# Computing the gMLP v projection tile by tile inside the norm loop, in an eight-core decoder layer

## What is computed

```python
h = rmsnorm(x, g_mix)
proj = h @ w_in                       # 1024 -> 3584
a = proj[..., :512]                   # pooling branch
z = gelu(proj[..., 512:1536])         # u: 512..1023, v: 1024..1535
u, v = z[..., :512], rmsnorm(z[..., 512:], g_v)
s = tril(w_s) @ v (per chunk of 128 tokens and group) + b_s
merged = gate_a * (pool(a) @ w_pool_out) + gate_b * ((u * s) @ w_gmlp_out)
x = x + merged @ w_out
x = x + (silu(h2 @ w_gate) * (h2 @ w_up)) @ w_down    # h2 = rmsnorm(x, g_ffn)
y = rmsnorm(x, g_final)
```

## Time and profile before

| | |
|---|---|
| median of 3 runs | 941.32 us (940.83 to 941.81) |
| the profiled execution | 941.41 us |
| its span on the slowest core (core 5) | 939.9 us |
| spans of the 8 cores | 933.0 to 939.9 us |
| PE busy | 858.1 us, 91% of the span |
| DVE, ACT, POOL busy | 360.4, 239.0, 151.4 us |

### The profile page before, as it was taken

How to read it: one execution, slowest core, us unless ns; L and a number is a source line. 1 busy time by engine, 2 the same in 40 slices (tenths; PEclk the granted TensorE clock), 3 DMA queues, 4 the chain that set the end, 5 groups by cost and what they waited for, 6 DMA issues and landing times.

```text
span 939.9 us, 13183 instructions; the slowest of 8 cores (933.0 to 939.9 us)
## 1 busy us (share of the span) xinstructions
PE 858.1 (91%) x4648; PEld 403.2 (43%) x4648; DVE 360.4 (38%) x594; ACT 239.0 (25%) x440; POOL 151.4 (16%) x174
## 2 busy tenths in 40 slices
PE   0589999998999999999972799999989999999996
PEld 0344444444444444444422344444444444444442
DVE  1584234447212112153456562343462212223446
ACT  2336222216221111100035272222072111110003
POOL 4202011015101100000034020110240110100004
PEclk9999999999999999999995899999989999999998
DMA  8992336676475573465489025366764646535404
GB/s 223 168 136 23 47 35 77 79 97 74 50 85 66 70 89 45 70 90 64 71 210 241 1 26 66 51 85 89 91 81 54 85 56 85 79 51 84 79 1 180
DMA packets 101795, 78.84 MB, mean 84 GB/s; under 512 B 5276, under 2 KB 96788, under 8 KB 101715
## 3 DMA queue, kind: packets, MB, share of 16 engines
q0 software_dynamic: 93936, 57.97, 48.2%
q1 hardware_dynamic: 6958, 19.31, 6.5%
q10 hardware_dynamic: 837, 0.72, 0.3%
HBM read 127.41 MB, written 9.01 MB: 145 GB/s over the span
## 4 chain that ended last, share of the span: by engine, by line
PE 83%; DMA 6%; DVE 4%; POOL 3%; issue 2%; ACT 1%; DVEq 0%; POOLq 0%; ACTq 0%; SPq 0%
PE ps L338 79%; DMA ring<-w_in 4%; POOL rs L356 2%; DMA yp<-ybuf 2%; PE ps L603 1%; PE ps L387 1%; PE ps L600 1%; DVE hb L375 1%; DVE shr L470 1%; DVE shr L474 1%; DVE shr L478 1%; DVE ovl L487 0%; ACT junk L347 0%; DVE ms L352 0%; ACT hT L395 0%
## 5 line engine op out<-in xcount | busy, mean ns | idle before, releaser
L338 PE MATMUL ps<-hT,ring 128*128 128x512 bf16 (+1 forms) x2720 | 503.7, 341 | 3.1 <-DMA ring<-w_in 3.1
L338 PEld LDWEIGHTS ps<-hT,ring 128*128 128x128 bf16 x2720 | 229.1, 98 | 263.4 <-issue 15.5
L338 PE MATMUL ps<-ring,ovl 128*128 128x512 bf16 (+1 forms) x1020 | 223.6, 379 | 0.0
L721 DVE TENSOR_TENSOR ovl<-ftmp,ps 128x512 bf16<-128x512 f32 (+1 forms) x110 | 62.4, 583 | 257.2 <-PE ps L338 250.9
L338 PEld LDWEIGHTS ps<-ring,ovl 128*128 128x128 bf16 (+1 forms) x1020 | 97.7, 97 | 120.7 <-issue 5.6
L714 ACT ACTIVATE ftmp<-ps 128x512 f32<-128x512 f32 (+1 forms) x110 | 56.6, 514 | 249.5 <-PE ps L338 249.5
L347 ACT ACTIVATE junk<-xbuf 128x1024 bf16<-128x1024 f32 (+1 forms) x51 | 53.7, 1054 | 203.5 <-DVE xbuf L741 139.3
L741 DVE TENSOR_TENSOR xbuf<-xbuf,ps 128x512 f32<-128x512 f32 (+1 forms) x102 | 70.0, 686 | 81.2 <-PE ps L338 81.2
L356 POOL TENSOR_TENSOR rs<-ms,mhalf 128x1 f32<-128x1 f32 (+1 forms) x68 | 64.5, 951 | 142.9 <-DVE ms L352 142.8
L387 PE MATMUL ps<-ident_b,hb 128*128 128x128 bf16 (+1 forms) x272 | 27.4, 262 | 60.9 <-DVE ms L352 43.4
L338 PE MATMUL ps<-ovl,ring 128*128 128x512 bf16 (+1 forms) x320 | 63.2, 337 | 0.0
(11 more groups left out here) (71 smaller groups left out, 375.6 us busy)
## 6 DMA issues: line engine op xcount, KB each, us to landing
ring<-w_gate POOLq DMA_DIRECT2D x22, 512.0 KB, 8.7
ring<-w_up POOLq DMA_DIRECT2D x22, 512.0 KB, 10.7
xbuf<-xp SPq DMA_DIRECT2D x16, 512.0 KB, 10.5
ring<-w_in POOLq DMA_DIRECT2D x16, 512.0 KB, 9.4
ring<-w_down POOLq DMA_DIRECT2D x8, 1024.0 KB, 9.6
yp<-ybuf SPq DMA_DIRECT2D x16, 512.0 KB, 5.6
ring<-w_in POOLq DMA_DIRECT2D x6, 1024.0 KB, 24.1
ring<-w_out POOLq DMA_DIRECT2D x4, 1024.0 KB, 13.1
```

What stands on the lines that cost most here:

```text
L338: ins = e.matmul(out=out, lhsT=lhs_fn(i), rhs=rhs_fn(i), start=(i == 0), stop=(i == n - 1))
L721: P.op('dve', lambda e, bU=bU, fi=fi, f=f, c0=c0, W=W: e.tensor_tensor(out=actT[:, f, c0:c0 + W], in0=ftmp[:, fi, :W], in1=PS[bU][:, :W], ...
```

## The change

It does four things.

- `blocks`: in each half the v block (`cb` = 2) is first, then a (0), then u (1). Before it was a, v, u.
- The v stage is gone as a stage. Its work is added to the norm pipeline as three more steps with lags 4, 5 and 6: `c1` (projection, gelu, square), `c2` (L352, L356), `c3` (product into `vtok`). The v block is released after the last tile, and `ws_prep` follows.
- `pipeline` goes through the steps of a round from the last to the first. This holds for all three places that use it.
- `b4_list[g]()` is called after group g of the u stage.

```diff
         for s in range(NSUP):
-            for cb in (0, 2, 1):
+            for cb in (2, 0, 1):
                 blocks.append([(0, 8, 512, win_v[:, :, cb * 512:(cb + 1) * 512])])
...
             for i in range(n + max(lags)):
-                for si, lag in enumerate(lags):
-                    t = i - lag
+                for si in reversed(range(len(lags))):
+                    t = i - lags[si]
                     if 0 <= t < n:
                         steps[t][si]()
...
-            pipeline([norm_stages(slot, R, col0, gmix_rep, 'gmix') for (slot, R, col0) in tts], [0, 1, 2, 3])
+            cj, cslot, cres_ = ring_next()
+            wvC = slot_view(cslot, 0, 8, 512)
+            steps = []
+            for (slot, R, col0) in tts:
+                ns = norm_stages(slot, R, col0, gmix_rep, 'gmix')
+                box = {}
+
+                def c1(slot=slot, R=R, col0=col0, box=box, wvC=wvC, cres_=cres_):
+                    b = bank()
+                    P.op('pe', mm_group(PS[b][:R, :],
+                                        lambda i: hT[:, i, col0:col0 + R],
+                                        lambda i: wvC[:, i, :], 8),
+                         reads=cres_ + hT_res([slot]), writes=[('ps', b)])
+                    fi = nxt('ft', 2)
+                    P.op('act', lambda e: e.activation(out=ftmp[:R, fi, :], in_=PS[b][:R, :],
+                                                       func=AF.Gelu_apprx_tanh),
+                         reads=[], writes=[('ftmp', fi), ('ps', b)])
+                    k, sq, rsf = rstd_stages(ftmp[:R, fi, :], R, 512, [('ftmp', fi)])
...
+                    sq()
+
+                def c2(box=box):
+                    box['rsf']()
+
+                def c3(slot=slot, R=R, box=box):
...
+                        P.op('dve', lambda e: e.scalar_tensor_tensor(
+                            out=vtok[:R, slot, :], in0=ftmp[:R, fi, :], scalar=rs[:R, k:k + 1], in1=gv_rep[:R, :],
+                            op0=ALU.mult, op1=ALU.mult),
+                             reads=[('ftmp', fi), ('rs', k), 'gv'], writes=[('vtok', slot)])
...
+                steps.append(ns + [c1, c2, c3])
+            pipeline(steps, [0, 1, 2, 3, 4, 5, 6])
+            ring_release(cj)
             if s == 0:
                 ws_prep()
...
-            cj, cslot, cres_ = ring_next()
-            wv = slot_view(cslot, 0, 8, 512)
-            for ti, (slot, R, col0) in enumerate(tts):
...
-                if ti % 2 == 1 and ti // 2 < 4:
-                    b4_list[ti // 2]()
-            ring_release(cj)
-
             dj, dslot, dres = ring_next()
...
                              reads=['stmp', ('ftmp', fi)], writes=[('sgT', g, c0)])
+                b4_list[g]()
             ring_release(dj)
```

More of the change, by code:

```diff
@@ L436, in build_nc @@
             t0 = s * TPS
-            pipeline([norm_stages(slot, R, col0, gmix_rep, 'gmix') for (slot, R, col0) in tts], [0, 1, 2, 3])
+            cj, cslot, cres_ = ring_next()
[15 more added lines that the diff above has]
+                    k, sq, rsf = rstd_stages(ftmp[:R, fi, :], R, 512, [('ftmp', fi)])
+                    box['fi'] = fi
+                    box['k'] = k
+                    box['rsf'] = rsf
+                    sq()
+                def c2(box=box):
+                    box['rsf']()
+                def c3(slot=slot, R=R, box=box):
+                    fi = box['fi']
+                    k = box['k']
+                    if slot < 8:
+                        P.op('dve', lambda e: e.scalar_tensor_tensor(
+                            out=vtok[:R, slot, :], in0=ftmp[:R, fi, :], scalar=rs[:R, k:k + 1], in1=gv_rep[:R, :],
+                            op0=ALU.mult, op1=ALU.mult),
+                             reads=[('ftmp', fi), ('rs', k), 'gv'], writes=[('vtok', slot)])
+                    else:
+                        P.op('dve', lambda e: e.scalar_tensor_tensor(
+                            out=vout[:R, :], in0=ftmp[:R, fi, :], scalar=rs[:R, k:k + 1], in1=gv_rep[:R, :],
+                            op0=ALU.mult, op1=ALU.mult),
+                             reads=[('ftmp', fi), ('rs', k), 'gv'], writes=['vout'])
+                        P.op('dve', lambda e: e.tensor_copy(out=vtok[:R, slot, :], in_=vout[:R, :]),
+                             reads=['vout'], writes=[('vtok', slot)])
+                        P.dma('sp', lambda e: e.dma_start(out=nvs[:, :], in_=vout[:NSMP, :]), 'omisc',
+                              reads=['vout'])
+                steps.append(ns + [c1, c2, c3])
@@ L549, in build_nc @@
                       reads=['npsbuf'])
-            cj, cslot, cres_ = ring_next()
-            wv = slot_view(cslot, 0, 8, 512)
-            for ti, (slot, R, col0) in enumerate(tts):
-                b = bank()
-                P.op('pe', mm_group(PS[b][:R, :],
-                                    lambda i, col0=col0, R=R: hT[:, i, col0:col0 + R],
-                                    lambda i, wv=wv: wv[:, i, :], 8),
-                     reads=cres_ + hT_res([slot]), writes=[('ps', b)])
-                fi = nxt('ft', 2)
-                P.op('act', lambda e, b=b, fi=fi, R=R: e.activation(out=ftmp[:R, fi, :], in_=PS[b][:R, :],
-                                                                   func=AF.Gelu_apprx_tanh),
-                     reads=[], writes=[('ftmp', fi), ('ps', b)])
-                k = rstd_chain(ftmp[:R, fi, :], R, 512, [('ftmp', fi)])
-                if slot < 8:
-                    P.op('dve', lambda e, fi=fi, R=R, k=k, slot=slot: e.scalar_tensor_tensor(
-                        out=vtok[:R, slot, :], in0=ftmp[:R, fi, :], scalar=rs[:R, k:k + 1], in1=gv_rep[:R, :],
-                        op0=ALU.mult, op1=ALU.mult),
-                         reads=[('ftmp', fi), ('rs', k), 'gv'], writes=[('vtok', slot)])
-                else:
-                    P.op('dve', lambda e, fi=fi, R=R, k=k: e.scalar_tensor_tensor(
-                        out=vout[:R, :], in0=ftmp[:R, fi, :], scalar=rs[:R, k:k + 1], in1=gv_rep[:R, :],
-                        op0=ALU.mult, op1=ALU.mult),
-                         reads=[('ftmp', fi), ('rs', k), 'gv'], writes=['vout'])
-                    P.op('dve', lambda e, R=R, slot=slot: e.tensor_copy(out=vtok[:R, slot, :], in_=vout[:R, :]),
-                         reads=['vout'], writes=[('vtok', slot)])
-                    P.dma('sp', lambda e: e.dma_start(out=nvs[:, :], in_=vout[:NSMP, :]), 'omisc', reads=['vout'])
-                if ti % 2 == 1 and ti // 2 < 4:
-                    b4_list[ti // 2]()
-            ring_release(cj)
             dj, dslot, dres = ring_next()
```

## The result

| | before | changed |
|---|---|---|
| median | 941.56 us (10 runs) | 977.28 us (9 runs) |
| profiled execution | 941.41 us | 979.42 us |
| its span, slowest core | 939.9 us (core 5) | 977.3 us (core 1) |
| mean of the 8 spans | 936.0 us | 969.5 us |

What follows compares the result with a forecast made beforehand. It took the chain of waits as the bound, with PE waiting for every copy in the fused loop. Terms 14.9 + 3.5 (second half 4.3 less 0.8) + 2.4 + 0 = +20.8 us on 941.41 gave 962 us, range 950 to 983.

Steps and rivals of the forecast that it cites:

- the clock rival: Fused loops: PE's clock falls in the waits, +2.0 us per low tile; half the tiles low gives 979 us; chance 0.20.
- first half, to the merge: First half's fused loop, a and u stages: u stage ends at 123.9 instead of 108.94, +14.9 us, bounds 12 and 17.
- second half, to the merge: Second half's fused loop, a and u stages: u stage ends at 585.5 against 581.2, +4.3 us.
- end of the first half: First scaling there no longer stands behind an addition and starts earlier: about 0.8 us comes back.
- w_out, both halves: Reversed w_out pipelines: period 2.28 against PE's 2.34, a gain against a slower start; 0, between -2 and +2 us.
- last block, end: Last block of w_down: scaling waits for the mean just made, period 2.28 instead of 1.87 us; +2.4 us.
- The loop's step: Fused loop: PE waits for every copy; a tile takes 3.36 us with a DVE copy, 4.49 with an ACT copy.
- The hidden norm stage: First half: norm stage costs nothing before, under the weight transfer; the new loop starts at 40.4 with one tile transposed.
- The clock: Fused loops: low clock counted only at the start, 2.8 us in the first half and 2.4 in the second.
- The stall moved into the u stage: First half's u stage: PE runs out of banks waiting for DVE's pooling, 3.1 us, replacing the v stage's 3.45 us stall.
- The rival that copies are hidden: Fused loops: copies run ahead of PE, a tile costs 2.34 us, total 938.5 us; chance 0.07.

Runs made afterwards that it cites:

- e2: Kernel before, with the w_pool matmuls called after each group of the u stage instead of in the v stage: 940.54 us, ratio 1.0008.
- e5: Changed kernel, order still reversed, with projection, second and third fused steps one round later (lags 5, 6, 7): 952.98 us.
- e10: Changed kernel, order still reversed, with all copies into hT of the fused loop on DVE: 959.92 us.
- e6: Changed kernel with 4 filler matmuls of 512 columns, read by nobody, ahead of each tile's projection: 968.42 us.
- e1: Kernel before, with only the order of steps in a pipeline round reversed, at all three places: 954.6 us, ratio 1.0159.
- e3: Changed kernel with the load of gv_rep on a semaphore of its own: ratio 1.0391 to the kernel before, against 1.0385 without the edit.
- e12: Kernel before, v projection fused only in the second half, forward with c3 first, w_pool in the u stage in both halves: 934.75 us, ratio 0.9929.

## Why the prediction was right, and where it was wrong

The sign, the two main terms and their order were right, and 977.3 lies in the range of 950 to 983. But the forecast's own value, 962, was 15 us short, and the result is outside of its own bounds of 951 to 970. The range held only because it was stretched for the clock rival, which had a chance of 0.20, against the forecast's 0.71. Term by term, in the means of the table:

| term | forecast | measured | of it |
|---|---|---|---|
| first half, to the merge | +14.9 | -1.2 + 20.7 = +19.5 | clock 2.6 |
| second half, to the merge | +4.3 | +10.6 | clock 6.2 |
| end of the first half | -0.8 | -0.2 | |
| w_out, both halves | 0 | +1.0 + 1.0 | |
| last block, end | +2.4 | +1.6 | |
| sum | +20.8 | +33.5 | the slowest core +37.4 |

Of the 12.7 us between the sums 8.8 are the clock, as the filler run measures it, about 2 are w_out, and about 2 more lie in the first half, where the u stage of core 1 took 32.26 us and not the 30.5 of the sum. The 4 us by which the slowest core lost more than the mean belong to no step of the sum; 2.5 of them are its first projection, which started at 42.95 and not at 40.40. These starts scatter between cores in kernels with an unchanged front too (34.2 to 43.9 in e2).

- **The loop's step.** Right at the full clock: 3.36 and 4.49 us computed, 3.27 and 4.46 found. e5 and e10 show that what exceeds PE's own work in it is the wait for the copy.
- **The hidden norm stage.** Right. PE stood 20.5 us for the weights with one tile transposed, and in no order did the first half come below 78 us.
- **The clock.** This is the step that failed: the forecast put the low clock in the loop at nothing beyond the start, 2.8 and 2.4 us. I wrote "No row here shows a swing, so I give it 0.20". It swung: behind the first, 3 of the 8 projections of the first half's loop were wholly or partly at the low level, and 6 of 7 in the second half's; the loops' PEclk was 0.83 and 0.72. The filler run measures it at 9 us. The rival's price, half of the tiles low and 979 us, came close to the total by luck: its +17 for the clock was twice what was measured, and the total got there with other terms. Its mark (PEclk under 1 between 45 and 76 us) was the right one to look at. The Trainium skill, TensorE: Matmul & The Clock Gate, "A second HAM failure mode: psum-queue depth-cycling", describes a kernel in which PE idles briefly and often between groups of matmuls and its clock swings between the two levels. The trace agrees, with 0.72 and 0.83 where PE paused in every step and 0.98 once the pauses were filled. By that page the clock belonged into the forecast.
- **The stall moved into the u stage.** Right in size (3.1 forecast, 2.81 found), slightly wrong in place: PE stood ahead of the first `w_pool` matmul and not at a projection that had no bank. What I left out is the low clock behind it, a projection of 3.23 us; the u stage took 32.26 us, not 30.5.
- **The second half.** With the clock held up (e6) it is +4.4 where +4.3 was forecast. That is closer than its terms deserve: the measured value holds the gelu's table load of 1.28 us, which the sum did not have. The low clock adds 6.2.
- **w_out.** Forecast as 0 between -2 and +2 for both halves, found +2.0: at the bound. The period is as forecast, 2.3 us per tile on core 1; it is the slower start that was sized too small. The first tile's mean stands ahead of the second addition now and waits for ACT's square, so the second addition starts 2.50 us behind the first (238.73 to 241.23), where it started 1.72 behind it before (214.43 to 216.15):

```profile
241.12 0.15 DVE L352 TENSOR_SCALAR ms<-ss 128x1 f32<-128x1 f32 x1 [1.70 <-ACT junk L347]
```

- **The end.** +1.6 for +2.4. The period is 2.21 us, not 2.28, and the power beside an addition takes 0.55 us, as taken. The Trainium skill, GPSIMD Engine Reference, Specifications, says that POOL contends with a DVE instruction that has two inputs in SBUF. The trace agrees: 0.55 us beside an addition with one input in PSUM, 1.47 beside a scaling.
- **The rival that copies are hidden** (0.07) was refused by the order on PE, and the trace shows a wait at every projection.
- I had not asked what the reversed order costs the norm stage by itself. It is 6.6 us in the second half (e1). The sum for the fused loop did contain it, since the copy stood on the path there anyway.

What stays open: a gain of a microsecond or so from the semaphore of its own (e3) would not be seen in the scatter between cores, and whether `w_pool` in the u stage helps beside the fused second half (e12).

## What to carry to other kernels

Before work is fused into a pipeline, ask what that pipeline is hidden behind: the first norm stage was free under a weight transfer, and the same fusion that gains 4 us in the second half loses 8 to 21 in the first. In a software pipeline a lag counts only if something else stands between producer and consumer in the consumer's queue; reversed rounds take that slack away, one more round gives it back. And where PE is left with short pauses in each step, the clock belongs into the sum and not only into a rival.

## What the runs showed of the hardware

- The clock fell in a loop in which pauses of 0.94 us stood in turn with longer ones, mostly 1.7 to 3.3 us, and rose again within it: 8 matmuls of 512 columns took 1.89, 2.64, 3.00 and 3.57 us in one loop. 4 matmuls more per step, which nobody reads, made the second half's stretch 6.2 us shorter.
- A change of ACT's table cost 1.28 us (534.10 to 535.40), and in the changed kernel's second half it stood on PE's path.
- In e10, with pauses of 0.94 to 1.26 us in each step of the second half's loop, the granted clock was 1.00 on seven cores and 0.96 on one.
- The POOL operation on one column takes 0.55 us alone and beside an addition that reads PSUM, and 1.47 us beside a scaling whose two large inputs are in SBUF.
